# First four units of a two-layer hybrid decoder on one Trainium2 core: half of their products taken in fp32 straight from loaded weights, two more pieces of the start's modulation on VectorE, one modulation step moved up

## What is computed

```python
c_act = jax.nn.silu(c)
for l in range(DEPTH):                       # 2 layers
    mod = (c_act @ ada_w[l] + ada_b[l])[:, None, :]
    sh1, sc1, g1, sh2, sc2, g2 = jnp.split(mod, 6, axis=-1)
    h = rmsnorm(x, norm_mix_w[l]) * (1.0 + sc1) + sh1
    x = x + g1 * hybrid_mixer(h, ...)        # begins with proj = h @ w_in[l]
    h = rmsnorm(x, norm_ffn_w[l]) * (1.0 + sc2) + sh2
    x = x + g2 * (swiglu(h, ...) if l % 2 == 0 else moe_swiglu(h, ...))
return rmsnorm(x, final_norm_w)
```

## Time and profile before

| | |
|---|---|
| median of 3 runs | 1588.82 us (1588.61 to 1588.83) |
| the profiled execution's own time | 1589.61 us |
| its span, first to last instruction | 1586.9 us |
| mean granted TensorE clock | 0.978 of full |
| PE / DVE / ACT busy | 96% / 82% / 60% |
| memory traffic, mean over the span | 295 GB/s |

### The profile page before, as it was taken

How to read it: one execution, slowest core, us unless ns; L and a number is a source line. 1 busy time by engine, 2 the same in 40 slices (tenths; PEclk the granted TensorE clock), 3 DMA queues, 4 the chain that set the end, 5 groups by cost and what they waited for, 6 DMA issues and landing times.

```text
span 1586.9 us, 26455 instructions
## 1 busy us (share of the span) xinstructions
PE 1528.8 (96%) x9638; PEld 1322.0 (83%) x9638; DVE 1294.7 (82%) x1508; ACT 957.9 (60%) x1104; POOL 39.5 (2%) x46
## 2 busy tenths in 40 slices
PE   6899999899999899999889999999999999999997
PEld 5898999899999898999877777777777777777775
DVE  7776878767764878868669989899899998989897
ACT  3434544444433533544368777787878777787784
POOL 0000000000000000000002000000000000000200
PEclk7899999999999999999979999999999999999999
DMA  9943878468976543789549999999999999999993
GB/s 348 295 143 107 264 254 287 152 194 293 305 300 196 167 144 128 259 287 375 194 124 385 395 388 396 383 377 370 382 364 388 372 379 381 363 386 368 392 391 147
DMA packets 260624, 469.00 MB, mean 296 GB/s; under 512 B 15732, under 2 KB 129580, under 8 KB 260548
## 3 DMA queue, kind: packets, MB, share of 16 engines
q1 hardware_dynamic: 257024, 456.75, 81.3%
q0 software_dynamic: 3248, 11.11, 1.9%
q10 hardware_dynamic: 276, 0.09, 0.0%
HBM read 453.90 MB, written 14.00 MB: 295 GB/s over the span
## 4 chain that ended last, share of the span: by engine, by line
PE 75%; DVE 4%; issue 1%; ACT 0%; DVEq 0%
PE psU L621 52%; PE psA L621 22%; PE psA L1033 1%; DVE split L1332 1%; DVE merged L1441 0%; PE psU L971 0%; PE psU L993 0%; DVE rstd L1437 0%; DVE split L1813 0%; DVE adacc L1404 0%; DVE sc L1567 0%; DVE work L1635 0%; DVE work L2017 0%; DVE work L1551 0%; DVE work L1544 0%
## 5 line engine op out<-in xcount | busy, mean ns | idle before, releaser
L1116 ACT ACTIVATE split<-raw 128x1024 fp32r<-128x1024 f32 x754 | 787.5, 1059 | 364.8 <-PE psU L621 180.3
L1813 DVE TENSOR_TENSOR split<-raw,split 128x1024 fp32r<-128x1024 f32 x528 | 615.2, 1219 | 22.7 <-ACT split L1116 20.7
L621 PE MATMUL psU<-hS,split 128*128 128x256 f32 x3936 | 490.2, 287 | 18.1 <-DVE hS L1518 14.7
L621 PEld LDWEIGHTS psU<-hS,split 128*128 128x128 f32 x3936 | 483.5, 195 | 20.9 <-issue 16.8
L621 PE MATMUL psU<-split,xE 128*104 128x512 f32 (+1 forms) x2304 | 498.1, 376 | 2.3 <-DVE xE L1940 2.3
L621 PEld LDWEIGHTS psU<-split,xE 128*104 128x104 f32 x2304 | 366.9, 168 | 120.2 <-issue 2.4
L1332 DVE TENSOR_TENSOR split<-raw,split 128x1024 fp32r<-128x1024 f32 x226 | 268.8, 1218 | 67.3 <-ACT split L1116 66.9
L621 PE MATMUL psA<-split,hidE 128*104 128x512 f32 x1056 | 249.2, 395 | 0.0
L621 PEld LDWEIGHTS psA<-split,hidE 128*104 128x104 f32 x1056 | 175.4, 168 | 63.9
L1404 DVE SCALAR_TENSOR_TENSOR adacc<-raw,cact,adacc 128x1024 f32<-128x1024 f32 x70 | 89.7, 1281 | 4.1
L621 PE MATMUL psU<-yS,split 128*128 128x256 f32 x576 | 70.1, 283 | 0.0
(11 more groups left out here) (241 smaller groups left out, 806.8 us busy)
## 6 DMA issues: line engine op xcount, KB each, us to landing
raw<-in_moe_w_dram SPq DMA_DIRECT2D x528, 512.0 KB, 7.0
raw<-in_w_in_dram SPq DMA_DIRECT2D x120, 512.0 KB, 5.9
raw<-in_ada_w_dram SPq DMA_DIRECT2D x96, 512.0 KB, 7.1
raw<-in_ffn_w_dram SPq DMA_DIRECT2D x66, 512.0 KB, 6.4
raw<-in_w_o_dram SPq DMA_DIRECT2D x16, 512.0 KB, 9.1
token_rows<-sc SPq DMA_DIRECT2D x10, 512.0 KB, 9.5
raw<-in_w_br_a_dram SPq DMA_DIRECT2D x8, 512.0 KB, 8.7
raw<-in_w_br_c_dram SPq DMA_DIRECT2D x8, 512.0 KB, 9.2
```

What stands on the lines that cost most here:

```text
L621: return pe.matmul(o, a, b, start=start, stop=stop, skip_group_check=True)
L1116: return act.activation(o, i, ACT.Copy)
L1813: TTN(split[:, slot, 1, :], raw[:, (RAW0 + n) % RAW, :], split[:, slot, 0, :].bitcast(F32), ALU.subtract).then_inc(s_lo, 1)
```

## The change

- `c` is loaded first, by itself, and transposed by itself; the other parameters are transposed behind `x`. The sigmoid and the product with `c` follow at once.
- The upper halves of the four units' weights are loaded into four buffers of their own (`whole`, in `work`) and not into the ring. PE multiplies them as fp32, 8 matmuls a unit in place of 24 fp32r ones and without high and low parts. ACT writes the first four chunks of h as fp32 into `merged` and then copies them to `hS`; DVE takes their low parts with two instructions of 512 columns in place of four of 256.
- These four loads stand between the first eight and the second eight pieces of the modulation, outside the ring, so that the second eight come four ring places earlier.
- The second half of the columns has no DIRECT pieces: eight pieces on DVE in place of six.
- The four products of section 2 that DVE did in two pairs among the first units stand together behind the turning of the gating weights. The high and low parts around the four units run less far ahead.
- `modulate` of section 7 stands in the iteration of the last but one hidden tile.

```diff
-DIRECT = [(1, 0, 2), (0, 0, 2), (1, 1, 3), (0, 1, 3)]
+DIRECT = [(1, 0, 2), (0, 0, 2)]
 PRODUCTS = [piece for piece in START if piece not in DIRECT]
 START_GROUPS = HEAD_GROUPS[:2]
+START_UNITS = [(0, g, j) for g in START_GROUPS for j in range(2)]
...
-            used += 5 if (kind, key[2]) == (START_GROUPS[0], 0) else 1
+            used += 1
...
-        out += [("split", "w_in", 0, h * 512, COLS[g] + 256 * j, 256) for g in START_GROUPS for j in range(2)]
+        if h:
+            out += [("split", "w_in", 0, h * 512, COLS[g] + 256 * j, 256) for g in START_GROUPS for j in range(2)]
...
+            if g == "f" and l:
                 out += two[:4]
+            if g == "ab" and l == 0:
+                out[-2:] = two[:2] + out[-2:] + two[2:4]
             if g == "u":
                 out += two[4:]
...
+                if pos == WHOLE_AT:
+                    for n in range(4):
+                        if n == 0:
+                            sp.wait_ge(s_rows, 1)
+                        src = w_in[0, 0:512, COLS[START_GROUPS[n // 2]] + 256 * (n % 2):COLS[START_GROUPS[n // 2]] + 256 * (n % 2 + 1)]
+                        sp.dma_start(whole(n).rearrange("p (k n) -> p k n", k=4), src.rearrange("(k p) n -> p k n", p=P)) \
+                            .then_inc(s_whole[n], 16)
...
+                bank = psA[2 * (EVENT_AT["half", h] % 2) + 1 - s]
+                first = (s, h) not in [piece[:2] for piece in DIRECT]
+                pe.wait_ge(s_afree, max(i for i, piece in enumerate(PRODUCTS) if piece[:2] == (s, h)) + 1)
+                for m in range(4):
+                    last = mm(bank[:, m:m + 1], acc[:, (4 * h + m) * P:(4 * h + m + 1) * P], ones[:, 0:1],
+                              first, m == 3)
+                    first = False
+                last.then_inc(s_half if s else s_ev, 1)
...
+                for n, key in enumerate(keys):
+                    banks.append(open_unit(key))
+                    pe.wait_ge(s_whole[n], 16)
+                    for m in range(2):
+                        for k in range(4):
+                            if n == 0 and m == 0 and k % 2 == 0:
+                                pe.wait_ge(s_hf, k // 2 + 1)
+                            mm(banks[n][:, m * T:(m + 1) * T], whole(n)[:, k * 256 + m * P:k * 256 + (m + 1) * P],
+                               merged[:, k, :], m == 0 and k == 0, False)
+                    if n == 2:
+                        open_event(("half", 1))
+                        half_section(1, 1)
+                half_section(0, 1)
+                for n, key in enumerate(keys):
+                    w = next_split()
+                    for m in range(2):
+                        for kk in range(4):
+                            if n == 0 and m == 0 and kk % 2 == 0:
+                                pe.wait_ge(s_h, 2 + kk // 2 + 1)
+                            last = tile(banks[n][:, m * T:(m + 1) * T], w, 4 + kk, kk * 256 + m * P, False, kk == 3)
+                    last.then_inc(s_used, 1)
...
-                    ada_half(1, 0)
-                    row_factors()
-                    ada_half(0, 0)
+                    bank, _ = open_event((0, "norm1"))
+                    open_event(("half", 0))
+                    direct_piece(0)
+                    half_section(1, 0)
+                    direct_piece(1)
+                    row_factors(bank)
+                    half_section(0, 0)
...
+                upto = used + (3 if key in START_UNITS else AHEAD)
...
+            act.dma_start(stackC[0:KD, :], c.rearrange("b (r p) -> (b r) p", p=P)).then_inc(s_c, 16)
...
+            act.activation(cact[:, :], unit("c")[:, 0:KD], ACT.Sigmoid).then_inc(s_cact, 1)
+            for j in range(4):
+                copy(xT[:, 2 * j:2 * j + 2, :].rearrange("p a b -> p (a b)"), unit(("x", j))[:, :]).then_inc(s_uA, 1)
             copy(vecs[:, :], unit(("vec", 0))[:, 0:NA_ROWS + NB_ROWS]).then_inc(s_uA, 1)
...
-                    act.wait_ge(s_eD, emptied(EVENTS, EVENT_AT["half", 0, h], "D"))
+                    high_parts(h)
+                    act.wait_ge(s_eD, emptied(EVENTS, EVENT_AT["half", h], "D"))
                     for k in range(4 * h, 4 * h + 4):
                         act.wait_ge(s_xr, k + 1)
-                        ins = act.activation(hS[:, 0, k, :], merged[:, k, :], ACT.Identity, bias=mod[:, 0, k:k + 1])
+                        ins = act.activation(hS[:, 0, k, :] if h else merged[:, k, :], merged[:, k, :], ACT.Identity,
+                                             bias=mod[:, 0, k:k + 1])
                         if k % 2:
-                            ins.then_inc(s_hh, 1)
-                    high_parts(4)
+                            ins.then_inc(s_hh if h else s_hf, 1)
+                    for k in (0, 2) if h == 0 else ():
+                        act.wait_ge(s_hf, k // 2 + 1)
+                        copy(hS[:, 0, k:k + 2, :].rearrange("p a b -> p (a b)"),
+                             merged[:, k:k + 2, :].rearrange("p a b -> p (a b)")).then_inc(s_hh, 1)
+                high_parts(4)
...
+                upto = used + (2 if key in START_UNITS else AHEAD - 1)
...
+            TTN(cact[:, :], cact[:, :], unit("c")[:, 0:KD], ALU.mult).then_inc(s_uD, 1)
...
+            def lower_bounds():
...
-                start_products(range(3))
+                start_products(range(2))
+                dve.wait_ge(s_uA, 5)
+                TTN(lbs[:, 1, 1, :], vecs[:, LB_ROW + HB:LB_ROW + 2 * HB], vecs[:, LB_ROW:LB_ROW + HB],
+                    ALU.subtract).then_inc(s_lbsig, 1)
+                start_products(range(2, 5))
...
-                start_products(range(3, 5))
+                start_products([5])
                 modulate_half(1, 0)
                 dve.wait_ge(s_eA, emptied(EVENTS, EVENT_AT[(0, "norm1")], "A"))
-                dve.wait_ge(s_uA, 5)
                 start_chunks(0)
-                start_products([5])
                 modulate_half(0, 0)
-                low_parts(1)
-                norm_low(0, 0, 0)
-                norm_low(0, 0, 2)
-                low_parts(4)
-                start_products(range(6, 11))
+                lower_bounds()
+                start_products(range(6, 9))
+                for k in (0, 2):
+                    dve.wait_ge(s_hh, k // 2 + 1)
+                    TTN(hS[:, 1, k:k + 2, :].rearrange("p a b -> p (a b)"), merged[:, k:k + 2, :].rearrange("p a b -> p (a b)"),
+                        hS[:, 0, k:k + 2, :].rearrange("p a b -> p (a b)").bitcast(F32), ALU.subtract).then_inc(s_h, 1)
+                start_products(range(9, 14))
                 modulate_half(1, 1)
                 start_chunks(1)
-                start_products([11])
                 modulate_half(0, 1)
-                low_parts(5)
+                low_parts(1)
                 norm_low(0, 0, 4)
...
-                    low_parts(8)
-                    for k in range(2):
-                        product(2, k)
+                    low_parts(4)
...
-                if l == 0:
-                    for k in range(2, 4):
-                        product(2, k)
...
                     turn_gating()
+                    low_parts(8)
+                    for k in range(4):
+                        product(2, k)
...
                 bank = unit(("ffn", f))
+                if f == NF - 2:
+                    modulate(FFN_ADA[-1])
...
             ffn_low(NF - 1)
-            modulate(FFN_ADA[-1])
```

More of the change, by code:

```diff
@@ L690, in ada_sum @@
                 last.then_inc(s_unit if s in DOWN_ADA else s_ev, 1)
-            def ada_half(s, h):
-                acc = ada1 if s else adacc
-                n = next(n for n, piece in enumerate(DIRECT) if piece[:2] == (s, h))
-                late = DIRECT[n][2] == 3
-                pos = MOD_POS[n]
-                bank, _ = open_event(("half", s, h))
-                def sums(ms, first, end):
-                    pe.wait_ge(s_afree, max(i for i, piece in enumerate(PRODUCTS) if piece[:2] == (s, h)) + 1)
-                    for m in ms:
-                        last = mm(bank[:, m:m + 1], acc[:, (4 * h + m) * P:(4 * h + m + 1) * P], ones[:, 0:1],
-                                  first and m == 0, end and m == 3)
-                    return last
-                def direct(first):
-                    pe.wait_ge(s_cact, 1)
-                    pe.wait_ge(s_cm, 1)
-                    pe.wait_ge(s_raw[pos % RAW], 16 * (pos // RAW + 1))
-                    for kk in range(2):
-                        for m in range(4):
-                            last = mm(bank[:, m:m + 1], raw[:, pos % RAW, (4 * kk + m) * P:(4 * kk + m + 1) * P],
-                                      cact[:, 2 * DIRECT[n][2] + kk:2 * DIRECT[n][2] + kk + 1],
-                                      first and kk == 0 and m == 0, False)
-                    last.then_inc(s_mpc, 1)
-                if late:
-                    sums(range(3), True, False)
-                    direct(False)
```

(21 more changed lines are left out.)

98 lines of the change are left out of this document (49 added, 49 removed).

## The result

The change takes 1574.22 us (median of 4 runs, 1573.68 to 1576.61) against 1588.82 (4 runs, 1588.61 to 1589.64): a ratio of 0.9909, with a 95% interval of 0.9896 to 0.9922. That is 14.6 us less; the prediction was 1574.8. The profiled execution took 1573.68 us, the shortest of the four. One execution of the kernel before, in a later series, took 2171 us at a mean granted clock of 0.652 and is left out of every comparison.

A forecast was written before the change was run, and what follows sets the result against it. PE, busy for 96% of the span, was taken as the bound. The start's 9.9 us plus section 7's 4.1 gave 14.0: 1589.6 profiled to 1575.6, less 0.8 for the median, 1574.8; range 1571.5 to 1581.0.

The forecast's parts named there:

- Part 1: Start to first upper half: first DVE product at 8.0 in place of 11.88, PE starts at 23.5 against 29.37.
- Part 2: Upper halves: 32 fp32 matmuls replace 96 fp32r ones, near 0.45 each; PE pays 0.6 us more per unit.
- Part 3: Second half of columns: DVE's products end at 38.7, PE's sum at 42.5; lower halves start at 44.7, not 53.00.
- Part 4: Lower halves and handover: end at 58.2 against 67.16; unit ab0 starts at 59.3 in place of 69.19, 9.9 us.
- Part 5: Section 7's modulation before the down projection: 2.4 us of wait and 1.7 of half clock go, together 4.1 us.
- The sum: 9.9 us from the start plus 4.1 from section 7, 14.0 us less; forecast 1574.8, chance 0.62.
- (a): DVE falls behind after the four products; PE waits at ac0 or level 2; gain 4.1 less, 1578.9; chance 0.14.
- (b): At the down projection PE waits for something else or DVE's last tiles come later; gain 4.1 less, 1578.9; chance 0.10.
- (c): Start shortened little: late `c`, fp32 at 0.5 or more, added DVE waits; within 3.2 us of before; chance 0.05.
- (d): Slower: clock stays at 1.2 GHz from the first fp32 matmul through the lower halves; +7.5, 1596.3; chance 0.05.

The follow-up runs named there:

- the second profile: The changed kernel run again unaltered, in a later series beside other versions: 1575.53 us (5 runs), ratio 0.9912 to the kernel before.
- 2.9 alone: The kernel before with only the modulation of section 7 moved ahead of the last two hidden tiles: 1586.25 us, ratio 0.9980, 2.9 us less.
- 4.1 as the last step: The changed kernel with the modulation of section 7 put back to its old place: 1578.31 us, ratio 0.9930, 4.1 more than the change.

## Why the prediction was right, step by step

**Part 1** was right in its numbers (8.0 and 23.5 against 7.74 and 23.86), not in one bound. A late `c` was priced at 1.5 us of PE's start, carried over from DVE one to one. The late `c` cost 0.14 there. The cover is the 2.00 us for which DVE waits at 21.03 for what comes from PE. `c` itself was there early, as assumed: in the second profile PE begins to transpose it at 2.56.

**Part 2** was right. Sixteen records took 3.70 us, 0.46 a product against the 0.45 by interpolation, and the half clock lasted 4.3 us into this work (23.9 to 28.2) against 5.2. The half clock's length is not a fixed sum, though: in the second profile it lasted 3.6 us into this work. The Trainium skill (FP8 and Floating Point Precision, TensorE Precision Notes) gives true FP32 four passes; at 0.125 us a pass that is an estimate of 0.50, and the trace gives less for this shape. What fp32 multiplication by itself gains or costs here was not measured: no run has the four buffers of their own and still multiplies the upper halves as fp32r.

**Part 3** was right in its number (44.7 against 43.99) and failed in its sentence "So DVE, not the loads, sets this". That holds for the products, which ended at 38.0, not for the lower halves. In the prediction's own figures PE's sum (42.5) was later than DVE's chunks (40.8), and the time of the lower halves was taken from PE's sum, so the number came right in spite of the sentence. The run with the DIRECT pieces back on PE shows the bound (DVE's work less by 3.3 us, the lower halves later by 3.75), and the sum in the middle of the unit shows it from the other side.

**Part 4** was 1.4 us too small: 11.3 against 9.9. Half of that, 0.7, is the earlier sum; the lower halves were 0.3 shorter; the rest is the handover, 0.6 us from their end to ab0 against the 1.1 allowed. The wait for q0 went because the products moved, as the run with these put ahead shows. The stretch at half clock of 3.4 us that was expected behind the idle time is in both profiles of the change: 3.4 us, and 13.23 and 13.24 us for the 96 matmuls. By the rule in the Trainium skill (TensorE: Matmul & The Clock Gate, HAM oscillation) only longer pauses do harm. The traces here disagree in part: 2.27 us idle had the stretch behind it in both profiles of the change, 0.43, 0.69 and 1.18 us had none, and at the down projection 2.7 us had it each time; but 2.40 us ahead of ab0, in the run with the products ahead of q0, had none. So a pause of that length can bring the stretch and need not, and what decides it stays open.

**Part 5** was right in its mechanism and 0.2 us too large in its size: 4.1 predicted, 3.9 by the traces at equal pace (2.4 for the wait, 1.5 for the stretch). That the medians say 2.9 alone and 4.1 as the last step is more the scatter of pace and clock between executions than a difference of the part.

**The sum** was 14.0; the spans differ by 15.0, the medians by 14.6. What was too small in part 4 (1.4) and the 0.85 us in the norm were partly taken back by the slower matmuls in the down projection (about 1.0). Neither of these two was in the prediction. Both vary between executions of one program: the change's second profile has 284 matmuls in that window and its first 281, and in the norm the second loses 1.3 us against the first. That the time came out within 0.6 us is therefore partly luck; the steps at the start, each within 0.8 us up to the lower halves, are not.

**The rivals.** (a) did not occur: the first of the two low parts for ac0 was written 2.3 us ahead, as counted.

```profile
69.37 2.35 DVE L1359 TENSOR_TENSOR split<-raw,split 128x1024 fp32r<-128x1024 f32 x2
...
72.92 6.00 PE L641 MATMUL psU<-hS,split 128*128 128x256 f32 x48
```

The first of these two ends near 70.6, and PE asks for it at 72.92. (b) would have needed a new wait in front of the down projection, and none is there. (c) fell with the first product at 7.74 and the first upper half at 23.86. (d) fell at 28.2, where the clock rose. But the fear behind it was not empty: in the run with the DIRECT pieces back the clock fell again for 6.8 us, and with the added matmuls it was down for 17 us on end.

## What to carry to other kernels

Ask of each join which side waits: a bracket on DVE's modulation told that PE was the bound, when the busy shares said nothing, and moving one sum into the middle of a unit then gave 3.7 us more (3.1 of it seen right behind the first units). A pause of PE between 2 and 3 us cost its length and mostly, not always, some 1.5 us of half clock behind it, so close or shorten those first, and give both prices. Put the loads that PE needs first ahead of the ones that it needs later, even where the later ones are on the longer chain: that place alone was worth 6.2 us at the lower halves.

## What the runs showed of the hardware that was not expected

- The pace of matmuls at full granted clock differs between executions. In the same stretch of the down projection 33.5 us held 288 matmuls in two of the thirteen traces (before, and the version with twenty-one added matmuls), 284 or 285 in six and 281 or 282 in five, some 2.4% from end to end. The change, run twice, had 281 and 284. What sets it isn't settled; the half clock ahead of it doesn't (285 with and without).
- The stretch at 0.50 in the norm ahead of the feed-forward part was 6.8 us long in the first profile of the change and 10.2 in the second, with the same program. From the end of the pause in it to the down projection the second took 1.3 us more, so a difference of 1 us between two orders can be that alone.
- A pause of 2.27 us ahead of the lower halves had a stretch at 0.50 behind it in both profiles of the change; in the run with the products ahead of q0 the same pause had it too, and one of 2.40 us, 16 us later, had none.
- PE can be shown busy for 17.00 of 17.00 us with the clock at 0.50 throughout (the run with the added matmuls, 11.0 to 28.0). A busy share says little of which clock one will get.
- An fp32 matmul of 256 columns costs 0.44 to 0.46 us at full clock, some 3.7 times an fp32r one of that size (0.12). Three fp32r matmuls (0.36) are cheaper for PE, so by these prices the exchange pays only where ACT, DVE or the ring, and not PE, is short. That is reckoned; no run here made the exchange alone.
